# Second layer's softmax session: query tiles from last to first, causal mask added by GpSimd to the decay rows

## The reference

```python
def forgetting_attention(q, k, v, log_f_cum):
    ...
    for i in range(s // Q_BLOCK):
        q0, q1 = i * Q_BLOCK, (i + 1) * Q_BLOCK
        logits = jnp.einsum("bqhd,bkhd->bhqk", q[:, q0:q1], k[:, :q1]).astype(jnp.float32) * scale
        decay = c[:, :, q0:q1, None] - c[:, :, None, :q1]
        ...
        logits = jnp.where(qpos >= kpos, logits + decay, -jnp.inf)
        p = jax.nn.softmax(logits, axis=-1).astype(v.dtype)
        outs.append(jnp.einsum("bhqk,bkhd->bqhd", p, v[:, :q1]))
```

## Time and profile before

| | |
|---|---|
| runs, device time | 1815.6, 1816.52, 1816.91 us |
| the profiled execution, first to last instruction | 1815.0 us |
| TensorE busy | 1782.3 us (98%) |
| VectorE busy | 1096.4 us (60%) |
| ScalarE busy | 732.8 us (40%) |
| GpSimd busy | 40.7 us (2%) |
| session b, first scores to last values | 1297.6 to 1404.9 us |
| granted TensorE clock, mean | 0.997 |

### The profile page before, as it was taken

The page is one execution under the profiler, slowest core; times in us unless marked ns, Lnnn a source line. Parts: engine busy times, 40 slices in busy tenths (PEclk is TensorE's granted clock), DMA queues, the critical chain, the costliest instruction groups (busy, mean ns, idle before and its releaser), DMA issues.

```text
span 1815.0 us, 22458 instructions
## 1 busy us (share of the span) xinstructions
PE 1782.3 (98%) x8312; PEld 1428.5 (79%) x8312; DVE 1096.4 (60%) x1601; ACT 732.8 (40%) x1031; POOL 40.7 (2%) x78
## 2 busy tenths in 40 slices
PE   7999999999999999999999999999999999999998
PEld 6887556788888888878888888889766788888887
DVE  6977775655555335775677774245577567767423
ACT  6313664344334323444444443232365443443322
POOL 4110000000000000000000000000000000000000
PEclk9999999999999999999999999999999999999999
DMA  9793112223322323312332222323401233222231
GB/s 356 251 337 136 47 53 93 82 93 101 107 93 87 97 94 94 115 48 93 105 104 92 92 92 87 104 85 107 163 24 47 70 108 100 92 92 92 93 105 70
DMA packets 149082, 195.29 MB, mean 108 GB/s; under 512 B 3647, under 2 KB 133001, under 8 KB 146333
## 3 DMA queue, kind: packets, MB, share of 16 engines
q1 hardware_dynamic: 141272, 155.28, 26.3%
q0 software_dynamic: 7600, 39.13, 5.8%
q10 hardware_dynamic: 148, 0.05, 0.0%
HBM read 189.15 MB, written 5.29 MB: 107 GB/s over the span
## 4 chain that ended last, share of the span: by engine, by line
PE 93%; DVE 4%; ACT 1%; issue 1%; DMA 0%; SPq 0%; ACTq 0%; DVEq 0%
PE bank L809 21%; PE bank L810 21%; PE bank L811 21%; PE bank L872 3%; PE bank L874 2%; PE bank L873 2%; PE bank L1454 2%; PE bank L1452 2%; PE bank L1453 2%; PE bank L948 2%; PE bank L965 1%; PE bank L996 1%; PE bank L852 1%; PE bank L853 1%; PE bank L854 1%; PE bank L1047 1%
## 5 line engine op out<-in xcount | busy, mean ns | idle before, releaser
L1922 DVE TENSOR_TENSOR w_lo<-w_stage,w_hi 128x2048 fp32r<-128x2048 f32 (+3 forms) x135 | 296.7, 2198 | 439.6 <-ACT w_hi L1480 439.5
L809 PE MATMUL bank<-act_hi,w_hi 128*128 128x512 f32 x1232 | 482.0, 391 | 1.6 <-DVE act_lo L1972 0.7
L811 PE MATMUL bank<-act_hi,w_lo 128*128 128x512 f32 x1232 | 479.5, 389 | 0.0
L810 PE MATMUL bank<-act_lo,w_hi 128*128 128x512 f32 x1232 | 479.4, 389 | 0.0
L1480 ACT ACTIVATE w_hi<-w_stage 128x2048 fp32r<-128x2048 f32 (+3 forms) x137 | 251.7, 1837 | 456.6 <-PE bank L811 334.6
L809 PEld LDWEIGHTS bank<-act_hi,w_hi 128*128 128x128 f32 x1232 | 231.2, 188 | 53.4 <-DVE act_lo L1972 2.3
L811 PEld LDWEIGHTS bank<-act_hi,w_lo 128*128 128x128 f32 x1232 | 231.2, 188 | 48.3
L810 PEld LDWEIGHTS bank<-act_lo,w_hi 128*128 128x128 f32 x1232 | 231.3, 188 | 47.7 <-issue 0.5
L809 PE MATMUL bank<-mid_hi,w_hi 128*128 128x512 f32 x352 | 136.9, 389 | 0.0
L810 PE MATMUL bank<-mid_lo,w_hi 128*128 128x512 f32 x352 | 136.9, 389 | 0.0
L811 PE MATMUL bank<-mid_hi,w_lo 128*128 128x512 f32 x352 | 136.9, 389 | 0.0
(11 more groups left out here) (412 smaller groups left out, 2612.3 us busy)
## 6 DMA issues: line engine op xcount, KB each, us to landing
ada_stage<-in_w_ada POOLq DMA_DIRECT2D x24, 1024.0 KB, 7.2
w_stage<-in_w_up SPq DMA_DIRECT2D x22, 1024.0 KB, 5.0
w_stage<-in_a_ffn_in SPq DMA_DIRECT2D x22, 1024.0 KB, 5.1
w_stage<-in_b_ffn_in SPq DMA_DIRECT2D x22, 1024.0 KB, 5.0
w_stage<-in_w_in SPq DMA_DIRECT2D x10, 1024.0 KB, 7.3
w_stage<-in_b_ffn_out SPq DMA_DIRECT2D x10, 1024.0 KB, 5.0
w_stage<-in_w_down SPq DMA_DIRECT2D x8, 1024.0 KB, 5.0
w_stage<-in_a_ffn_out SPq DMA_DIRECT2D x8, 1024.0 KB, 5.1
```

The costliest lines, as they stand in the source:

```text
L809: pe.matmul(dst, wh, mh, start=start and k == 0, stop=False)
L810: pe.matmul(dst, wh, ml, start=False, stop=False)
L811: last = pe.matmul(dst, wl, mh, start=False, stop=stop and k == nk - 1)
L1922: dve.tensor_tensor(w_lo[slot][:, 0:n], raw[:, 0:n], w_hi[slot][:, 0:n].bitcast(FP32), ALU.subtract).then_inc(w_ready, 1)
```

## The change

Three things change. First, session b takes the query tiles of each pair from the last to the first: a causal pair's units have 512, 384, 256 and 128 keys. Second, the mask product L954 is gone; GpSimd adds `causal_neg` to the diagonal block of each head's decay row in place, 48 additions of 128x128, so that `shift_scores` adds the mask with the decay. Before it, a unit with more keys must have read the row, since there this block stands unmasked: GpSimd waits for the `shift_scores` of the unit before (but in a pair's first unit), and VectorE's `shift_scores` waits for the addition (`decay_masked`). Third, what hung on the number of the unit now hangs on the query tile, or on "first" and "last" of the pair; in the last pair tiles 1 to 3 are multiplied when tile 1 is done, and tile 0 at the end.

```diff
@@ p_of, buffers by query tile @@
-        def p_of(u, h):
-
+        def p_of(x, h):
+
+            u, qi = x["u"], x["qi"]
...
@@ session, the order of the units @@
-                for qi in range(NT):
-                    units.append(dict(d, pair=PAIR0[name] + p, u=UNIT0[name] + 4 * p + qi, qi=qi,
+                for n in range(NT):
+                    qi = NT - 1 - n if name == "b" else n
+                    units.append(dict(d, pair=PAIR0[name] + p, u=UNIT0[name] + 4 * p + n, qi=qi,
                                       n=P * (qi + 1) if causal else NMEM, causal=causal,
-                                      mask=causal and name == "b", last=qi == NT - 1,
+                                      masked=4 * (p - 2) + n if causal and name == "b" else None,
+                                      first=n == 0, last=n == NT - 1,
...
@@ GpSimd, behind the load of the decay rows @@
+            pool.wait_ge(decay_back, 16)
+            for x in session("b"):
+                if x["masked"] is None:
+                    continue
+                block = slice(P * x["qi"], P * (x["qi"] + 1))
+                for h in range(2):
+                    if not x["first"]:
+                        pool.wait_ge(scores_read, 2 * (x["u"] - 1) + h + 1)
+                    row = decay[:, 2 * (x["masked"] // 4) + h, block]
+                    pool.tensor_tensor(row, row, causal_neg[:, :], ALU.add).then_inc(decay_masked, 1)
...
@@ TensorE, scores @@
-                    last = pe.matmul(dst[h][:, 0:n], x["q"][rows, P * qi:P * (qi + 1)],
-                                     x["k"][rows, 0:n], start=True, stop=True)
-                    if not x["mask"]:
-                        last.then_inc(scores_ready, 1)
-                if x["mask"]:
-                    for h in range(2):
-                        pe.matmul(dst[h][:, P * qi:P * (qi + 1)], ident_b[:, :], causal_neg[:, :],
-                                  start=False, stop=True, skip_group_check=True).then_inc(scores_ready, 1)
+                    pe.matmul(dst[h][:, 0:n], x["q"][rows, P * qi:P * (qi + 1)], x["k"][rows, 0:n],
+                              start=True, stop=True).then_inc(scores_ready, 1)
...
@@ TensorE, value_tiles @@
+                if x["u"] >= UNIT0["b"]:
+                    return [0] if x["last"] else [1, 2, 3] if x["qi"] == 1 else []
...
@@ ScalarE and VectorE, save_pT @@
-                if x["qi"] == 0 and x["pair"]:
+                if x["first"] and x["pair"]:
...
@@ VectorE, shift_scores and b_beside @@
+                if x["masked"] is not None:
+                    dve.wait_ge(decay_masked, 2 * x["masked"] + h + 1)
...
-                if t == 8:
-                    dve.wait_ge(decay_back, 16)
```

More of the change, by code:

```diff
@@ L263, in cells_of @@
             return (cells_a if u >= UNIT0["mem_a"] else cells_0)[h]
-        def p_of(u, h):
+        def p_of(x, h):
+            u, qi = x["u"], x["qi"]
             if UNIT0["mem_a"] <= u < UNIT0["b"]:
                 return p_ring_a[:, u % RING, h, :]
-            if u % 4 == 3:
+            if qi == 3:
                 return (p_high_b if u >= UNIT0["b"] else p_high_0)[:, h, :]
-            if u % 4 == 0 and u >= UNIT0["b"]:
+            if qi == 0 and u >= UNIT0["b"]:
                 return p_mem_b[:, h, :]
-            return cells_of(u, h)[:, P * (7, 10, 13)[u % 4]:]
+            return cells_of(u, h)[:, P * (7, 10, 13)[qi]:]
         def pt_step(x):
@@ L412, in program @@
             sem("f_plus"), sem("f_summed"), sem("f_saved"))
-        tri_set, bf_loaded, decay_stored, decay_back = (
-            sem("tri_set"), sem("bf_loaded"), sem("decay_stored"), sem("decay_back"))
+        tri_set, bf_loaded, decay_stored, decay_back, decay_masked = (
+            sem("tri_set"), sem("bf_loaded"), sem("decay_stored"), sem("decay_back"), sem("decay_masked"))
         y_tile, y_added, y_gained, gain_loaded = (
@@ L983, in values @@
                 qi = tiles[0]
-                if qi == 0 and (pair > PAIR0["b"] or 0 < pair < PAIR0["mem_a"]):
+                opens = 3 in tiles if pair >= PAIR0["b"] else qi == 0
+                if opens and (pair > PAIR0["b"] or 0 < pair < PAIR0["mem_a"]):
                     pe.wait_ge(out_saved, pair)
-                elif qi == 0 and pair == PAIR0["b"]:
+                elif opens and pair == PAIR0["b"]:
                     pe.wait_ge(group_free, G0["b_q"] + 1)
-                elif qi == 0 and pair == PAIR0["mem_a"]:
+                elif opens and pair == PAIR0["mem_a"]:
                     pe.wait_ge(group_free, G0["a_q"] + 1)
-                elif qi == 0 and pair == PAIR0["mem_a"] + 1:
+                elif opens and pair == PAIR0["mem_a"] + 1:
                     pe.wait_ge(scores_read, 2 * UNIT0["b"] - 2)
                 end = P * (tiles[-1] + 1)
-                for kj in range(x["n"] // P):
+                for kj in range(tiles[-1] + 1 if x["causal"] else NMEM // P):
                     q0 = P * (max(qi, kj) if x["causal"] else qi)
@@ L1007, in softmax @@
                     x, y, z = (unit_at(units, t - lag) for lag in (0, TURN_LAG, VALUE_LAG))
-                    if x and name == "b" and x["qi"] == 0 and t >= 8:
+                    if x and name == "b" and x["first"] and t >= 8:
                         pe.wait_ge(q_saved, t // 4 - 1)
@@ L1526, in exps @@
                 c = (2 * u + h) % 8
-                p = p_of(u, h)[:, 0:n]
+                p = p_of(x, h)[:, 0:n]
                 act.activation(p, p, ACT.Exp, scale=-1.0, bias=neg_max[:, c:c + 1],
```

6 lines of the change are left out of this document (3 added, 3 removed).

## The result

The changed kernel takes 1819.53 us (median of 11 runs, 1818.1 to 1822.28) against 1816.35 us before (11 runs): a ratio of 1.0017, 95% interval 1.001 to 1.0025. Forecast were 1815.5 us and a range up to 1819.0. The profiled execution took 1818.94 us, with a span of 1817.2 us, 2.2 more than before.

What follows compares the result with a forecast made beforehand. TensorE, busy 98% of the span, was taken to bound steps 8 to 26, with waits for copies in steps 27 to 31. Terms of -1.3 and +0.3 gave -1.0 us: 1815.5 us, range 1812.0 to 1819.0.

Steps and rivals of the forecast that it cites:

- masks removed: TensorE's stream, steps 8 to 26: 19 causal units each lose a mask cost of 0.10 us, 1.9 us less.
- order: Reversed units in session b: 1.30 us later at step 26's quarter, 0.09 later after it, 0.66 and 0.14 less behind.
- additions: GpSimd's additions in steps 28 to 31 delay normalizations: 0.3 us more, with 0 and 1.2 as the ends.
- work ahead of the quarter's end: TensorE up to step 26's quarter: scores and transposes of 512 keys replace those of 128, 0.64 and 0.66 us more.
- late-mask rival: VectorE waits for `decay_masked` in each unit with a unit before it: about 1822 us, chance 0.04.
- that hides two additions of 0.4: Steps 8 to 26: VectorE's 3.7 us to spare in a pair hide two additions of 0.4 us, not of 1.3.
- The second rival: GpSimd's additions hold up VectorE throughout: 1825.5 us at 0.6 us each, 1835 at 0.8; chance 0.08.
- its point of decision, 0.46 us: Addition length from which VectorE held up by GpSimd decides: 3.7 us spare in a pair over 8 additions.
- the wait of the copy of 512: Step 27: VectorE's copy of 512 keys waits for the values of the pair before, taken as 0.3 us.
- the longer last transposes: TensorE before the values of step 31: four transposes of the last head, not one, 0.33 us.
- the five others: Causal units outside steps 8 to 26, whose mask cost falls in steps where TensorE waits anyway.
- first rival: TensorE's waits in steps 27 to 31 go, so 2.5 us come in full and up to 1.8 more: 1812.2 us, chance 0.10.

Runs made afterwards that it cites:

- no masks: Kernel before, forward order, with the mask products left out of TensorE's stream and put nowhere else: 1814.76 us, ratio 0.9995.
- reversed order with the clock held by the fillers: Changed kernel without additions and masks, plus 13 unused matmuls in TensorE's idle time of steps 27 to 31: 1816.78 us, ratio 1.0005.
- plus the additions: Changed kernel, GpSimd's additions included, plus 13 unused matmuls of 512 columns in steps 27, 29, 30 and 31: 1818.30 us, ratio 1.0009.
- without additions: Changed kernel without GpSimd's additions and VectorE's wait for them, no causal mask put anywhere: 1818.66 us, ratio 1.0011.
- the two forward runs: Kernel before, 1816.35 us, and the same kernel with its mask products left out, 1814.76 us.
- the doubled additions: Changed kernel with each GpSimd addition followed by a second one, of zeros, onto the same block: 1821.67 us, ratio 1.0027.
- the kernel with gap and late split: Changed kernel with the step without a projection quarter moved to the fourth unit and four split quarters to steps 31 to 34: 1820.32 us, ratio 1.0018.

## Why the prediction was wrong

The runs form a chain in which one thing changes at a time: before; no masks; reversed order with the clock held by the fillers; plus the additions; less the fillers, which is the changed kernel. Its steps in us of session, against the prediction's terms:

| term | predicted | measured | by medians of time |
|---|---|---|---|
| masks removed | -1.9 | -1.19 | -1.7 |
| order | +0.6 | +1.39 | +2.0 |
| additions | +0.3 | +1.31 | +1.4 |
| clock | none | +1.52 | +1.5 |
| sum | -1.0 | +3.03 | +3.2 |

The predicted order term is 1.30 (work ahead of the quarter's end) and 0.09 (steps 27 to 31), less 0.80 (behind). The profiles are single ones. The medians agree, but each ratio above has an interval of about 0.09% (1.6 us) to either side, so they bear out the sum more than its parts. Two steps were measured twice: the additions also as 1.32 (with the falling clock), the clock also as 1.51 (without additions).

**The clock** is the largest part, and the prediction had no step for it. It read 1.00 in the rows of before and carried that over, though it had TensorE's work in steps 27 to 31 going down and VectorE, with an unchanged set of work, setting the time: TensorE had to idle more, just ahead of its longest pieces.

**The additions.** Their length was right (0.43 us, forecast 0.4 from the earlier trace rows), and that VectorE waits for `decay_masked` hardly at all was right, so the late-mask rival fell. (The VectorE instruction of the earlier trace rows reads one tile as both of its inputs, and not two tiles; the reading of the wait stays the same.) Wrong was "that hides two additions of 0.4": the step divided VectorE's 3.7 spare us of a pair by eight additions. Most of that spare lies in the fourth unit, where TensorE is busy for 5 us; the third has none, and there 0.2 us on a normalization, or on two in a row, reach TensorE through the copy or the eviction behind it. The windows of the third and the fourth unit after, steps 18 and 19 (VectorE's busy time is the third figure behind the length):

```profile
1349.90:1352.71 2.81, 2.48 (x14) 1.64 (x13) 2.81 (x10) 2.81 (x8) 1.12 (x4) 1.00 0.02 6
1352.71:1357.90 5.19, 5.19 (x36) 3.34 (x35) 2.89 (x11) 2.20 (x7) 0.70 (x2) 1.00 0.00 0
```

Of the 1.31 us, 0.77 fall ahead of step 27, where the prediction had nothing. The second rival named the mechanism, but its point of decision, 0.46 us, rested on the same average. Nor does the cost go by the time that GpSimd works: on balance the doubled additions cost nothing more ahead of the values, since what counts is whether an addition runs beside a normalization that TensorE waits for.

The Trainium skill (SBUF — State Buffer, section Who interferes with whom) says that of VectorE and GpSimd the one that starts first keeps the shared ports for its instruction. As to which instructions are held up the trace agrees: normalizations grow by 0.17 us and more, while score reads, with one input in PSUM, stay at 0.67 to 0.69 us for 512 keys. Of the addition the Trainium skill (GPSIMD Engine Reference, section Elementwise — side-by-side cycle accounting) let me estimate 0.28 us and the dispatch; measured are 0.43.

**The order.** Step 27 comes 1.09 us later than without the reversal (81.82 against 80.73), where 1.30 - 0.66 = 0.64 was forecast. TensorE's step 22 shows most of it: without a quarter it has 0.94 us of work (0.63 for the scores of 256 keys, 0.31 for two transposes), and it takes 1.45 even without additions, with a wait for VectorE's copy in it. Steps 27 to 31 cost 0.26 us more than the forecast against that point (2.10 - 1.09 and not 1.39 - 0.64), and 0.71 came back behind, forecast 0.80. What the 0.26 us consist of was not separated. The mechanisms of this step were right: the split earlier behind the quarter's end (3.45 us and not 3.98, forecast 0.54 less), the wait of the copy of 512, the longer last transposes.

**The masks.** The 0.10 us came from one pair of rows. From step to step of the two forward runs it is 0.05 to 0.09, and 19 times 0.07, less a new wait of 0.21 us for an eviction in step 13, is about what was measured. That the five others are hidden was right.

That the waits of steps 27 to 31 would go (first rival) fell: they grew from 1.5 to 4.4 us.

## What to carry to other kernels

Spare time of an engine counts only in the step where the delay falls; an average over a pair hides a step that has none. Before work is taken from TensorE in a stretch that another engine paces, ask what its idle time does to its clock: here 1.5 us of the 3.0 were nothing but that, and thirteen filler matmuls won them back. And take work from the engine that sets the pace: moving four split quarters of VectorE's by four steps won 2.4 us in the forward order, where removing 48 mask products from TensorE in this way lost 3.2.

## What the hardware showed

Behind TensorE's waits of 0.64, 1.07, 0.44 and 1.05 us in steps 29 to 31 the granted clock fell to its lower level for most of the next 4 us (0.54 and 0.61 in windows of 2 us), with windows of 0.50 in the kernel with gap and late split; eight transposes went from 1.09 to 1.97 us, sixteen value products from 2.38 to 3.12. The mean clock of a profile does not show it: 0.997 before and 0.998 after. In the profile of before the clock also fell near 20 and 205 us (0.69 and 0.76 in windows of 5 us), far from the change. A GpSimd addition of 128x128 onto the decay rows takes 0.42 us alone and up to 0.87 beside VectorE, and a pair of normalizations beside it 0.17 to 0.35 us longer than without.
